# A planner that puts dots and sums ahead of the streams' steps, with the coefficient as its own step and units of one slot

## The reference: what is computed

```
h  = rms_norm(x) @ w_in                 # split into attention, indexer and retention parts
A  = attention over the top-256 keys per query, by indexer scores
       sum_h w_h * relu(q_h . k)        # causal; the sample reads paged caches
B  = retention in chunks of 128, group norm, times silu(gate)
x += concat(A, B) @ w_out
n  = rms_norm(x)
# PEER: 8 heads; per head top-16 of 128 keys in two halves, then top-16 of the 256 pairs
hval = u_emb[eid] . n                   # 128 experts (slots) per token
x += sum over slots of softmax(score) * gelu(hval) * v_emb[eid]
y  = rms_norm(x)
```

## Time and profile before

| | us |
|---|---|
| median of 3 runs | 3858.67 (3858.39 to 3861.91) |
| the profiled execution | 3870.04 |
| its span, first to last instruction | 3868.2 |
| TensorE matmul busy | 3178.7 (82%) |
| VectorE busy | 2674.1 (69%) |
| ScalarE busy | 993.7 (26%) |
| GpSimd busy | 1237.8 (32%) |
| gathers of the lookup | 1056, 1128.34 MB on their queue |
| mean granted TensorE clock | 0.93 |

### The profile page before, as it was taken

The page is one execution under the profiler, slowest core; times in us unless marked ns, Lnnn a source line. Parts: engine busy times, 40 slices in busy tenths (PEclk is TensorE's granted clock), DMA queues, the critical chain, the costliest instruction groups (busy, mean ns, idle before and its releaser), DMA issues.

```text
span 3868.2 us, 31404 instructions
## 1 busy us (share of the span) xinstructions
PE 3178.7 (82%) x9551; PEld 1543.8 (40%) x9551; DVE 2674.1 (69%) x6543; ACT 993.7 (26%) x2512; POOL 1237.8 (32%) x1084
## 2 busy tenths in 40 slices
PE   5999864988798879887987898689887389879776
PEld 2444253443354325433543453245433144334321
DVE  1222138888868778978888888988856998434655
ACT  1111122152134214421432153115222022311211
POOL 0000001444444434443443344234342124333443
PEclk9999977999999999998999899899999699889999
DMA  4111133999999999999999999889998179988998
GB/s 170 57 66 50 54 116 134 391 417 397 392 404 407 415 370 369 394 399 361 397 400 368 364 385 408 341 341 384 356 394 340 70 297 420 392 338 343 414 421 341
DMA packets 190425, 1245.72 MB, mean 322 GB/s; under 512 B 22704, under 2 KB 27184, under 8 KB 50672
## 3 DMA queue, kind: packets, MB, share of 16 engines
q0 software_dynamic: 155520, 1128.34, 72.4%
q1 hardware_dynamic: 34736, 115.37, 7.9%
HBM read 1220.50 MB, written 22.46 MB: 321 GB/s over the span
## 4 chain that ended last, share of the span: by engine, by line
PE 44%; DMA 26%; DVE 24%; issue 3%; ACT 1%; SPq 1%; POOL 1%; DVEq 0%; ACTq 0%; POOLq 0%
PE yacc L1030 23%; DMA weights<-in_uv,eid 19%; PE bank L857 11%; DVE weights L1484 7%; DVE kv L1346 3%; DVE tiny L1345 3%; PE bank L993 3%; DMA weights<-in_w_out 2%; PE bank L967 2%; DVE weights L1416 1%; DVE weights L1215 1%; DVE weights L1412 1%; DMA kv<-in_cache_ik,gi 1%; POOL weights L1838 1%; ACT diag L1747 1%
## 5 line engine op out<-in xcount | busy, mean ns | idle before, releaser
L1030 PE MATMUL yacc<-weights,diag 128*128 128x512 f32 (+1 forms) x4224 | 2002.5, 624 | 364.7 <-ACT diag L1747 363.4
L1838 POOL DMA_INDIRECT weights<-in_uv,eid x1056 | 1210.5, 1146 | 2578.1 <-PE yacc L1030 1875.8
L1484 DVE CUSTOM_DVE_ANT_0 weights<-weights,xn 128x1024 f32<-128x1024 f32 x1056 | 1290.2, 1224 | 597.5 <-DMA weights<-in_uv,eid 585.8
L1030 PEld LDWEIGHTS yacc<-weights,diag 128*128 128x128 f32 (+1 forms) x4224 | 802.5, 196 | 1453.6 <-issue 909.3
L1747 ACT ACTIVATE diag<-main,coef 128x128 f32<-128x128 f32 x1024 | 356.7, 394 | 1450.8 <-DVE coef L1475 1381.1
L1345 DVE MAX8 tiny<-kv 128x8 f32<-128x384 f32 (+6 forms) x224 | 245.0, 1094 | 3.0
L1755 ACT ACTIVATE gl<-hv 128x2 f32<-128x2 f32 x528 | 107.1, 203 | 530.6 <-DVE hv L1484 529.9
L1346 DVE MATCH_REPLACE8 kv<-tiny,kv 128x384 f32<-128x384 f32 (+6 forms) x224 | 241.6, 1079 | 0.0
L967 PE MATMUL bank<-weights 128*128 128x512 f32 (+1 forms) x288 | 158.4, 687 | 87.0 <-DMA weights<-in_w_out 85.8
L857 PE MATMUL bank<-weights 128*128 128x512 f32 (+3 forms) x560 | 229.6, 572 | 0.0
L857 PE MATMUL bank<-weights,mid 128*128 128x512 f32 (+1 forms) x448 | 183.2, 570 | 0.0
(11 more groups left out here) (240 smaller groups left out, 2309.8 us busy)
## 6 DMA issues: line engine op xcount, KB each, us to landing
weights<-in_w_out SPq DMA_DIRECT2D x72, 512.0 KB, 7.8
weights<-in_uv,eid POOLq DMA_INDIRECT x1056, 9.8
Hb<-h_scratch SPq DMA_DIRECT2D x8, 1700.0 KB, 10.7
weights<-in_w_in SPq DMA_DIRECT2D x6, 2048.0 KB, 18.8
h_scratch<-Hb SPq DMA_DIRECT2D x4, 1700.0 KB, 5.5
h_scratch<-spare SPq DMA_DIRECT2D x4, 1700.0 KB, 5.5
nw<-in_wffn SPq DMA_DIRECT2D x9, 512.0 KB, 6.4
nw<-in_wfin SPq DMA_DIRECT2D x9, 512.0 KB, 14.3
```

Of the source, the lines that this page charges most:

```text
L1030: mm = nc.tensor.matmul(yacc[0:W, 512 * j:512 * (j + 1)], diag[:, n % 4, 0:W], ring[:, n % RING, D + 512 * j:D + 512 * (j + 1)], start=Fal ...
L1484: ins = V.tensor_tensor_reduce(u, u, xn[:, t % 2, :], 1.0, 0.0, ALU.mult, ALU.add, hv[:, n % RING:n % RING + 1])
L1838: pool.indirect_dma_start(dst, None, table, bass.IndirectOffsetOnAxis(ap=ids, axis=0)).then_inc(s, 16)
```

## The change

The list of steps is planned anew, and units are single slots.

- `PAIR` is 1: a gelu and a coefficient instruction for each slot, on one column.
- The coefficient and the diagonal become a step of their own, `weigh`, that is planned 0.75 after its dot, and `drain` goes.
- In the choice among steps that can start, `weigh` comes ahead of a dot, and dots and sums come ahead of all steps of the streams. They have no due times any more.
- Retention leaves the front and becomes a `side` stream per tile. The first half of the sample's key logits becomes a stream, `past`, and is no longer interleaved with rounds of the top-k by hand. Conditions in `candidates()` keep what depends on them behind them.
- `ycopy` of a tile is listed once the next tile's PEER keys are.
- On the chip, ScalarE's silu for the sample is tied to another part of `retained`, and GpSimd waits for the sample's gate (`gated`) ahead of the first key gather.
- `PERIOD` is 360 in place of 400, `LEAD` 100 in place of 150, `NEAR` 0.1 in place of 0.4, and the sample's front is due 200 later and spread over 0.8 of a period.

```diff
-PAIR = 2
+PAIR = 1
...
+def side_steps(t):
+    if t == SAMPLE:
+        steps = [Step("sdecay", t, 0, "P", 1.2, 1), Step("sdecayed", t, 0, "D", 4.5, 1, 0.3), Step("sret", t, 0, "P", 10.0, 1, 0.5),
+                 Step("retained", t, 0, "D", 2.3, 1)]
...
+        return steps + [Step("sstored", t, 0, "D", 0.2, 0, 6.0), Step("retained", t, 1, "D", 2.2), Step("retained", t, 2, "D", 2.6, 0, 0.8)]
+    return [Step("decay", t, 0, "P", 1.2, 1), Step("decayed", t, 0, "D", 2.3, 1, 0.3), Step("hold", t, 0, "P", 2.4, 1, 0.5),
+            Step("carry", t, 0, "P", 1.2, 0, 0.5), Step("carried", t, 0, "D", 1.4, 1, 0.3),
+            Step("retained", t, 0, "D", 2.3), Step("retained", t, 1, "D", 2.2), Step("retained", t, 2, "D", 2.6, 0, 0.8)]
...
+def past_steps():
+    return [Step("slogits", SAMPLE, (b, c), "P", 2.0, 1, 1.2 if c < 5 else 4.0) for b in range(4) for c in range(6)]
...
-PERIOD, LEAD, ROW, LATENCY, NEAR = 400.0, 150.0, 2.62, 3.4, 0.4
+PERIOD, LEAD, AHEAD, LATER, LAST, ROW, LATENCY, NEAR = 360.0, 100.0, 0.0, 200.0, 0.8, 2.62, 3.4, 0.1
...
-        if t in chosen and drained == t:
+        if due:
+            yield "D", dotted[due[0]] + 0.75, -2e7, "weigh"
+        if t in chosen:
             at = arrival(t, k)
             if at is not None:
-                yield "D", at, t * PERIOD + PERIOD * k / units(0), "unit"
-        if drained < t:
-            yield "D", dotted[drained, units(drained) - 1] + 0.8, -1e9, "drain"
+                yield "D", at, -1e7, "unit"
...
-            yield "P", weighed[t, k] + 1.0, t * PERIOD + PERIOD * k / units(0), "sums"
+            yield "P", weighed[t, k], -1e7, "sums"
+        if copying and (copying[0][0] == TILES or copying[0][0] + 1 in keyed):
+            yield "", copying[0][1], 0.0, "ycopy"
...
-            clock["D"] = start + PAIR * 1.32 + (0.18 if k else 0)
-            dotted[t, k] = clock["D"]
-            if k:
-                weighed[t, k - 1] = clock["D"] - 1.3
+            clock["D"] = dotted[t, k] = start + PAIR * 1.32
+            due.append((t, k))
...
+        elif kind == "weigh":
+            s.append(("weigh",) + due[0])
+            clock["D"] = start + 0.18
+            weighed[due.pop(0)] = start + 1.2
...
                     ins = V.tensor_tensor_reduce(u, u, xn[:, t % 2, :], 1.0, 0.0, ALU.mult, ALU.add, hv[:, n % RING:n % RING + 1])
-                    if k and s == PAIR * k:
-                        weigh_pair(t, k - 1)
                 ins.then_inc(hval_ready, 1)
...
             def unit(t, k):
-                if k:
-                    spread_pair(t, k - 1)
...
                 if b == 0:
+                    pool.wait_ge(gated, TILES + 1)
                     filled(pool, ("skT", NB - 1, 1))
```

More of the change, by code:

```diff
@@ L256, in front_steps @@
         steps = [Step("load", t, 0, "", 0, 1, 12.0), Step("sheads", t, 0, "P", 3.0, 1, 2.5), Step("spad", t, 0, "D", 4.0, 2, 0.3),
[L257 to L260, removed]
-            if k:
[L262 to L265, removed]
+                 Step("sturn", t, 0, "P", 2.3, 1), Step("sspread", t, 0, "D", 2.6, 1, 0.3), Step("swi", t, 0, "P", 2.8, 1, 0.4),
                   Step("swiT", t, 0, "D", 1.6, 1, 0.3)]
@@ L268, in front_steps @@
         steps += [Step("splace", t, 0, "D", 9.0, 1, 0.3)]
[L269 to L272, removed]
+        steps += [Step("topk", t, k, "D", 4.8, 0, 0.3) for k in range(ROUNDS)]
         steps += [Step("mask", t, 0, "D", 1.4, 0, 0.3)]
@@ L356, in make_schedule @@
     clock = {"P": 0.0, "D": 0.0}
-    fronts = [Stream(front_steps(t), (t - 2) * PERIOD - LEAD, PERIOD) for t in range(TILES + 1)]
-    backs = [Stream(back_steps(t), (t - 1) * PERIOD, 0.9 * PERIOD) for t in range(TILES + 1)]
-    front = back = 0
+    fronts = [Stream(front_steps(t), (t - 2) * PERIOD - LEAD + (t == SAMPLE) * LATER, PERIOD if t < TILES else LAST * PERIOD)
+              for t in range(TILES + 1)]
+    backs = [Stream(back_steps(t), (t - 1) * PERIOD - AHEAD, 0.9 * PERIOD) for t in range(TILES + 1)]
+    sides = [Stream(side_steps(t), (t - 2) * PERIOD - LEAD, 0.5 * PERIOD) for t in range(TILES + 1)]
+    pasts = [Stream(past_steps(), (SAMPLE - 2) * PERIOD + LATER, PERIOD)]
+    front = side = back = past = 0
     rows_at = 0.0
     chosen, keyed, mixed, seeded, finished, kept = {}, {}, {}, {}, {}, {}
-    dotted, weighed, summed = {}, {}, {}
-    dot, pair, drained = (0, 0), (0, 0), 0
+    turned, held, returned, placed = {}, {}, [], []
+    dotted, weighed, summed, copying = {}, {}, {}, []
+    dot, due, pair = (0, 0), [], (0, 0)
     def arrival(t, k):
@@ L375, in heads @@
             yield "front", fronts[front]
+        if side <= TILES and side in turned:
+            yield "side", sides[side]
+        if not past and placed and SAMPLE in held:
+            yield "past", pasts[past]
         if back <= TILES:
@@ L381, in candidates @@
             e = stream.head()
-            what, t, _ = e.entry
+            what, t, part = e.entry
             ready = stream.ready()
@@ L386, in candidates @@
                 continue
+            if what in ("decay", "sdecay"):
+                ready = max(ready, turned[t])
+            if what == "mixT" or (what, part) in (("attend", 3), ("sscores", 0)):
+                if t not in held:
+                    continue
+                ready = max(ready, held[t])
+            if what == "sturn":
+                if not returned:
+                    continue
+                ready = max(ready, returned[0])
+            if what == "slogits" and part == (0, 0):
+                ready = max(ready, held[t], placed[0])
+            if what == "smask" and part == (0, 0):
+                if not past:
+                    continue
+                ready = max(ready, pasts[0].ends[-1])
             if what == "mixT" and t:
@@ L424, in make_schedule @@
             start = max(clock[on], start)
-        if kind in ("front", "back"):
-            stream = fronts[front] if kind == "front" else backs[back]
+        if kind in ("front", "side", "back", "past"):
+            stream = {"front": fronts[front:], "side": sides[side:], "back": backs[back:], "past": pasts}[kind][0]
             e = stream.head()
@@ L439, in make_schedule @@
                 mixed[t] = end
+            if (what, part) in (("turn", 3), ("spad", 0)):
+                turned[t] = end
+            if what == "sret":
+                returned.append(end)
+            if what == "splace":
+                placed.append(end)
+            if what == "retained" and part == 2:
+                held[t] = end
             if stream.head() is None and kind == "front":
                 front += 1
+            elif stream.head() is None and kind == "side":
+                side += 1
+            elif stream.head() is None and kind == "past":
+                past += 1
             elif stream.head() is None:
@@ L1667, in silu @@
                 R = rows(t)
-                if part:
+                if part != (t == SAMPLE):
                     return
@@ L1737, in gate_exps, with spread @@
                 A.activation(g, g, ACT.Exp).then_inc(gate_exp, 1)
-            def spread_pair(t, k):
+            def spread(t, k):
                 select = ident if t < TILES else fold
@@ L1755, in unit @@
                 A.activation(gl[:, c:c + PAIR], hv[:, c:c + PAIR], ACT.Gelu).then_inc(gelu_ready, 1)
-            def drain(t, part):
-                spread_pair(t, units(t) - 1)
             def ycopy(t, part):
```

29 lines of the change are left out of this document (14 added, 15 removed).

## The result

The changed kernel takes 3971.43 us (3969.04 to 3976.07, four runs) beside 3860.29 us for the kernel before: a ratio of 1.0288, with an interval of 1.0271 to 1.0306. It is 111 us slower; 3780 was forecast, and 3885 was the upper end of the range. The profiled execution took 3969.04 us around a span of 3967.2.

What follows compares the result with a forecast made beforehand. Two limits were named: the transfers, and the order in which VectorE takes dots and other steps. Tiles 2 to 5 -35, tile 6 -114 and tail +70 give -79, from 3858.7 to 3780 us; range of 8 in 10, 3645 to 3885.

Steps and rivals of the forecast that it cites:

- tile 6, -114: Tile 6: dots between the sample's top-k rounds raise the DMA share from 0.77 to 0.99, 513 to 399 us.
- the wait of 84.7 us: GpSimd's wait in tile 6 for the weighted sum that would free a buffer; predicted to lose its cause.
- its lead of 77 us: The next tile's expert choice was ready 77 us ahead of its keys (2394.4 against 2471.6).
- Tiles 2 to 5, -35: Ready dots and sums going first: gain between 20 (VectorE limit) and 69 us (transfers at 0.99); 35 taken.
- the first of the text's signs of being wrong: The low-traffic stretch lies ahead of tiles 4 to 6, next choice late, instead of before the sample's gathers.
- the rival of starving streams: Planner prices leave streams 43% of a slot, not 54%; choices and sample come late; 3890 to 3950 us, chance 0.23.
- The tail, +70: End of kernel: sample's expert choice at 3685 against 3615, when tile 7's gathers make room; 70 us lost.
- the 333: Time in us the sample's 32 top-k rounds need when sharing VectorE with dots, instead of 186.
- Units of one slot, 0: 528 more gelus and coefficients: gelus hidden, coefficients 0.12 us each within VectorE's share, waits for gelus taken as 0.
- a sign that it would be wrong: VectorE's wait for the gelu rising from 15 us to hundreds would show the prediction wrong.
- The 40 us that the prediction worked out by it: If grouping helps saturated VectorE, added coefficients cost 10 us in each of four tiles, the sum 40 us higher.
- The moves costed at nothing: Retention and past-logit streams, GpSimd's wait for the sample's gate, and the sum's later copy: each costed at 0.

Runs made afterwards that it cites:

- the split run: The changed kernel's single-slot instructions in the list order planned for units of two slots, each pair's step written as two: 3923.72 us, 1.0163 of the kernel before.

## Why the prediction was wrong

The working forecast tiles 2 to 5 at -35, tile 6 at -114 and the tail at +70. By first dots of the table above, the profiled run lost 19.0 us up to tile 6 (2906.3 against 2887.3), 14.9 in tile 6 (528.3 against 513.4) and 66.1 in tile 7 with its tail (438.0 against 371.9); the sample's own gathers took 1.0 less. That is 99.0, the whole difference of the spans. Tiles 2 to 5 alone lost 27.3 (1556.0 against 1528.7 from the first dot of tile 2 to that of tile 6); 8.3 were gained ahead of them.

**The step that failed is tile 6, -114**: "with dots between the rounds the wait of 84.7 us has no cause". Dots can stand between the rounds only if there are dots. With dots ahead of all, tile 6's were finished before the sample's top-k began, and those of tile 7 couldn't exist, because the last steps that choose tile 7 (`pick`) stood behind that same top-k in the list. So the rounds ran bare: 155 us with no dot, where before 24 dots went among them. The claim is sound where its condition holds: with the sample 400 us later tile 7 was chosen first, and its dots went at a DMA share of 0.99 among 16 of the rounds. By due time the rounds ran bare as well (no dot among them at the sample's new time or at its old one), and tile 6 took 528 to 568 us. I had treated a choice as something that would always be there, by its lead of 77 us.

**Tiles 2 to 5, -35**, fail by the same step in a milder form. Within a tile the claim held: the dots of tiles 1 to 4 took 335 to 344.5 us, and GpSimd's longest wait for a free buffer was 34 us. But the lead was used up by tile 2, and 22, 28, 35, 49 and 66 us stand between the gathers of successive tiles up to tile 6; this is the first of the text's signs of being wrong, at more boundaries than it named. The lists that `make_schedule()` writes have it already: before, 86 to 100 of a tile's 128 slots stand ahead of the choice of the next tile (for tiles 1 to 7); after, 121 stand ahead of the choice of tile 1 and all 128 ahead of every later one. In the other runs, too, the stands for a choice begin where the list comes to 128, or to 127: from tile 6 on with pairs, from tile 5 on with low prices, and ahead of the sample alone by due time. The prediction had this mechanism as the rival of starving streams, with its cause in the prices, and gave it 0.23 and 3890 to 3950. The low and high prices show that cause at work (-72 and +92 us), and the line that ranks the dots shows the other half of it (-76). The price in the text was too small, since it counted the lost lead once and not in every tile, and the chance was too small as well: the place of each choice stood in the list before any run, so the growth from tile to tile could have been read off it.

**The tail, +70**, measured 66 with the change, but not for the reason given, so that the nearness is luck. The rounds weren't stretched among dots to 333 us but took 155 (the 333 is itself a little low: the text works out 54% of VectorE for them and then divides by 0.55, where 0.54 gives 339); the sample was chosen late because tile 7 was chosen late, and because the sample's streams were due 200 us later: with dots by due time, its old time gives 34 us back (1.0088 to 0.9995), and with dots ahead and low prices some 25 (1.0101 to 1.0031). The prediction had no term for that later time.

**Units of one slot, 0**, hold as instructions, and so does the 0.12 us a coefficient: VectorE's busy time grew by 64.2 us for 528 more. What the term left out is the plan, in which a slot of its own is priced at 1.50 us and one of a pair at 1.41: with dots ahead, the order planned for pairs was 48 us faster with the same instructions. VectorE's wait for the gelu rose from 14.6 to 163.9 us, which the text called a sign that it would be wrong; the same wait rose to 105 us in the old plan with single slots, which wasn't slower, so the sign was badly chosen. The rule weighed there, of the Trainium skill's "Perfetto Trace Analysis", section "Optimizing Scalar/DVE Operations", is that grouping can improve throughput if the engine is saturated. The 40 us that the prediction worked out by it didn't appear: 3921 us grouped against 3924 split, in one order, with VectorE busy 81% to 89% of each of tiles 1 to 5 in the split run.

**The moves costed at nothing** can be stated only together. The run by due time with the sample at its old time keeps the side and past streams, the later `ycopy`, the rank of the sums, single slots and new constants, and equals the kernel before (0.9995). As single slots gave 0.5% in the old plan, the rest may have cost that much; it wasn't taken apart. Nor was an order tried in which the sums go by due time.

So, undone in this order, the 111 us are 76 from the rank of the dots (1.0288 to 1.0088) and 34 from the later sample (1.0088 to 0.9995), with the rest together at nothing. The shares aren't fixed: the causes meet in one list. At the low prices the rank alone cost 45 and the later sample some 25, and with the rank kept the low prices gave 72 back and the order for pairs 48. Tile 6 takes over 510 us in every order but that with the sample 400 us later, where it takes 334 and tile 7's stretch 614: the sample's chain moves and doesn't vanish. No order was run that hides it.

## What to carry to other kernels

Before ranking the work that fills a queue over the work that produces its next batch, compute per batch how much of the producer fits between two consumers at the planner's prices, and carry the shortfall on from batch to batch; then count in the list, before any run, how many consumers stand ahead of the next batch's choice. Here the lead was gone by the second batch, and the engines follow the list. A price above the measured duration can make the order worse though no instruction changes; lowering a slot's from 1.50 to 1.25 us was worth 72 us with dots ahead and 32 without (there with the sample at its old time). The version to keep is dots by due time, low prices, single slots and the sample's old due time, at 0.9918 of the time before; the longest stand left in it is the 200 us in tile 6.

## What the runs showed of the hardware

An instruction on one column cost as much as on two (gelu 188 to 202 ns on one, 202 to 203 on two; coefficient 155 to 158 on one, 156 to 160 on two), and 1056 more such instructions in the same order moved the time by less than 3 us (3921 and 3924). GpSimd took the gathers in the order of its list: in the run by due time with the sample's old time and low prices, one page gather waited 138 us and no slot's gather went for 200 us, though tile 6 had been chosen 340 us before. In the longest stands the queue moved 55 and 60 GB/s, against 404 and 411 for the dots of tiles 6 and 7 with the sample 400 us later.
